# A two-layer decoder step on one core: squares summed before the product that averages them, gate rows in one pass, sample states outside the tiles

## The reference, cut to what matters

```
y = x * rsqrt(mean(x*x) + eps) * g                 # _rmsnorm, before every projection
proj = h @ w_in                                    # layer 0: 8 groups of 512 columns, and 8 gate columns
rq, rk, rv, rg, mq, mk, mv, mo, mi, mf = split(proj)
i_pre = mi + b_gates[:4];  log_f = log_sigmoid(mf + b_gates[4:])
S_new = S * chunk_dec + einsum('bhsk,bhsv->bhkv', kc * k_dec, vc)   # 4 retention heads
C_new = dec * C + einsum('bhsk,bhsv->bhkv', kc * w_end, vc)         # 4 mLSTM heads
x = x + concat(o_ret, h_m) @ w_out
x = x + swiglu(rmsnorm(x))                         # dense
# layer 1: HGRN2 mixer (8 heads), then top-2-of-8 SwiGLU experts on rmsnorm(x), then a last rmsnorm
```

## Time and profile before

| what | value |
|---|---|
| median of three runs | 1583.95 us (1582.96 to 1591.84) |
| span of the profiled execution | 1580.1 us, 23315 instructions |
| busy | PE 96%, PEld 84%, DVE 74%, ACT 58%, POOL 6% |
| granted TensorE clock, mean | 0.988 |
| DMA | 403.87 MB, mean 256 GB/s |

### The profile page before, as it was taken

How to read it: one execution, slowest core, us unless ns; L and a number is a source line. 1 busy time by engine, 2 the same in 40 slices (tenths; PEclk the granted TensorE clock), 3 DMA queues, 4 the chain that set the end, 5 groups by cost and what they waited for, 6 DMA issues and landing times.

```text
span 1580.1 us, 23315 instructions
## 1 busy us (share of the span) xinstructions
PE 1522.6 (96%) x8687; PEld 1333.2 (84%) x8687; DVE 1164.5 (74%) x1269; ACT 910.9 (58%) x905; POOL 87.7 (6%) x90
## 2 busy tenths in 40 slices
PE   6999998999999989998999999999999999999997
PEld 5888787999999988996778888888888888888885
DVE  5656566455454598686479898888988888898886
ACT  4334444434433544343277787877778787777773
POOL 0024100000000000102030000000000000000002
PEclk9999999999999999998999999999999999999999
DMA  7567723698545531444199999999999999999993
GB/s 206 149 112 142 144 74 94 184 301 261 144 129 153 180 103 54 127 132 142 64 384 359 402 391 364 386 360 390 379 388 384 364 385 363 398 386 372 393 353 126
DMA packets 214584, 403.87 MB, mean 256 GB/s; under 512 B 14467, under 2 KB 131503, under 8 KB 214386
## 3 DMA queue, kind: packets, MB, share of 16 engines
q1 hardware_dynamic: 203104, 372.82, 68.2%
q0 software_dynamic: 6208, 22.06, 4.5%
q10 hardware_dynamic: 5202, 8.03, 1.5%
HBM read 372.58 MB, written 30.28 MB: 255 GB/s over the span
## 4 chain that ended last, share of the span: by engine, by line
PE 86%; DVE 9%; ACT 2%; issue 1%; DMA 1%; ACTq 0%; DVEq 0%; SPq 0%
PE bank L483 25%; PE bank L484 24%; PE bank L485 24%; DVE dense_lo L1709 2%; PE bank L683 2%; PE bank L940 1%; PE bank L725 1%; PE bank L1089 1%; ACT dense_hi L1293 1%; PE bank L588 1%; DMA arena<-in_x_sample 1%; DVE w_lo L2218 1%; PE bank L675 1%; PE bank L620 1%; DMA ring<-in_w_in_c 0%
## 5 line engine op out<-in xcount | busy, mean ns | idle before, releaser
L2218 DVE TENSOR_TENSOR w_lo<-arena,w_hi 128x2048 fp32r<-128x2048 f32 (+1 forms) x280 | 597.1, 2166 | 84.7 <-ACT w_hi L1588 81.8
L1588 ACT ACTIVATE w_hi<-arena 128x2048 fp32r<-128x2048 f32 (+1 forms) x280 | 500.7, 1820 | 114.0 <-PE bank L485 113.0
L483 PE MATMUL bank<-w_hi,xg_hi 128*128 128x512 f32 (+1 forms) x768 | 287.5, 374 | 2.5 <-DVE w_lo L2218 2.3
L484 PE MATMUL bank<-w_lo,xg_hi 128*128 128x512 f32 (+1 forms) x768 | 286.1, 373 | 0.0
L485 PE MATMUL bank<-w_hi,xg_lo 128*128 128x512 f32 (+1 forms) x768 | 285.4, 372 | 0.0
L1709 DVE TENSOR_TENSOR dense_lo<-ring,dense_hi 128x2048 fp32r<-128x2048 f32 (+1 forms) x78 | 167.7, 2152 | 134.7 <-ACT dense_hi L1293 134.6
L1293 ACT ACTIVATE dense_hi<-ring 128x2048 fp32r<-128x2048 f32 (+1 forms) x78 | 140.6, 1804 | 179.4 <-PE bank L485 153.2
L483 PE MATMUL bank<-h_hi,dense_hi 128*128 128x320 f32 x512 | 170.2, 332 | 20.4 <-DVE h_lo_a L1715 7.8
L483 PEld LDWEIGHTS bank<-w_hi,xg_hi 128*128 128x128 f32 x768 | 144.5, 188 | 31.9 <-issue 4.3
L485 PEld LDWEIGHTS bank<-w_hi,xg_lo 128*128 128x128 f32 x768 | 144.2, 188 | 25.9
L484 PEld LDWEIGHTS bank<-w_lo,xg_hi 128*128 128x128 f32 x768 | 144.5, 188 | 24.9
(11 more groups left out here) (410 smaller groups left out, 2355.5 us busy)
## 6 DMA issues: line engine op xcount, KB each, us to landing
arena<-in_w_moe_down SPq DMA_DIRECT2D x176, 512.0 KB, 6.7
arena<-in_w_moe_gate SPq DMA_DIRECT2D x128, 512.0 KB, 6.7
arena<-in_w_moe_up SPq DMA_DIRECT2D x128, 512.0 KB, 7.0
arena<-in_w_moe_gate SPq DMA_DIRECT2D x64, 384.0 KB, 5.6
arena<-in_w_moe_up SPq DMA_DIRECT2D x64, 384.0 KB, 4.0
ring<-in_w_in_ab SPq DMA_DIRECT2D x32, 512.0 KB, 8.8
ring<-in_w_in_c SPq DMA_DIRECT2D x32, 512.0 KB, 4.7
expert_rows<-ZERO SPq DMA_DIRECT2D x12, 1024.0 KB, 8.2
```

The costliest lines, as they stand in the source:

```text
L483: mm(out, left[0], right[0], start=start, stop=False)
L484: mm(out, left[0], right[1], start=False, stop=False)
L1588: fn(WH[SLOT_OF[p]][:, 0:unit_size(p)], STAGE[:, s, 0:unit_size(p)], ACT.Copy).then_inc(S("unit_hi"), 1)
L2218: v.tensor_tensor(WL[w][:, 0:n], STAGE[:, s, 0:n], WH[w][:, 0:n].bitcast(F32), ALU.subtract).then_inc(S("unit_split"), 1)
```

## The change

- The eight squares of each norm are first summed on VectorE (`add_squares`, seven additions into tile 0; for n3 the first seven tiles, six additions), then one product (n3: two) with the 1/D matrix. The product's place is where the last two stood. The additions stand behind the low parts in VectorE's order, each waiting for the square and for the addition before it.
- `gates` makes one output of 36 rows: input gate columns at 0 to 3, forget gate columns at 32 to 35, zeros between. The two weight parts get a place in the arena that GpSimd zeroes at the start (two memsets); ScalarE fills the high part with two copies, VectorE the low part with two subtractions. ScalarE's `gate_rows` first copies the forget rows out of the bank, adds the bias to the input rows, then adds the bias to the forget rows in place.
- `along` is taken out before `state` of heads 0, 3, 4, 5 and 6. Their tile runs through, then the prompt's products, then the four sample products back to back.

```diff
-    silu0 mq3 along state0 wh wl wh state1 conv2 wl score2 ...
+    silu0 mq3 state0 wh wl wh state1 conv2 wl score2 ...
...
-    along weigh3 silu4 wl state2 conv4 mv0 conv5 mk3 along state3 conv6 wh silu5 shift4 wh mv1 ...
+    along weigh3 silu4 wl state2 conv4 mv0 conv5 mk3 state3 conv6 wh silu5 shift4 wh mv1 ...
...
-    conv7 center1 silu7 wl mv4 score4 mv5 mo0 weigh4 wh shift5 mo1 along state4 wl score5 wh center2 wl mo2
-    finish4 weigh5 finish5 center3 center4 conv_out rg0 along state5 center5 var0 root0 shift6 score6 mo3 weigh6
-    mix0 mix1 wh mix2 gate0 wl wh wl rg1 shift7 finish6 score7 mix3 gate1 rg2 along state6 rg3 along weigh7
+    conv7 center1 silu7 wl mv4 score4 mv5 mo0 weigh4 wh shift5 mo1 state4 wl score5 wh center2 wl mo2
+    finish4 weigh5 finish5 center3 center4 conv_out rg0 state5 center5 var0 root0 shift6 score6 mo3 weigh6
+    mix0 mix1 wh mix2 gate0 wl wh wl rg1 shift7 finish6 score7 mix3 gate1 rg2 state6 rg3 along weigh7
...
+            SUMMED = {"n1": 0, "n2": KD - 1, "n3": 2 * (KD - 1)}
...
             def mean_squares(tag):
                 b = open_bank("act")
+                if tag == "n3":
+                    pe.wait_ge(S("squares_summed"), SUMMED["n3"] + KD - 2)
+                    mm(b[:, 0:NT], C("inv_d"), SQF[tag][:, 0, :], start=True, stop=False)
+                    pe.wait_ge(S("n3_squares"), KD)
+                    ins = mm(b[:, 0:NT], C("inv_d"), SQF[tag][:, KD - 1, :], start=False, stop=True)
+                else:
+                    pe.wait_ge(S("squares_summed"), SUMMED[tag] + KD - 1)
+                    ins = mm(b[:, 0:NT], C("inv_d"), SQF[tag][:, 0, :], start=True, stop=True)
+                close_bank("act", ins, (tag, "ms"))
...
             def gates():
-                for r in range(2):
-                    b = open_bank("act")
-                    for k in range(KD):
-                        ins = product3(b[0:H4, 0:NT], [x[:, k, r * H4:(r + 1) * H4] for x in (WGH, WGL)],
-                                       [x[:, k, :] for x in HA], k == 0, k == KD - 1)
-                    close_bank("act", ins, ("gate", r))
+                b = open_bank("act")
+                for k in range(KD):
+                    ins = product3(b[0:GROW, 0:NT], [x[:, k, :] for x in (WGH, WGL)], [x[:, k, :] for x in HA],
+                                   k == 0, k == KD - 1)
+                close_bank("act", ins, "gate")
...
                     gemm_tile(w, k % 2 * P, src, "dve", (kind, k), KD)
-                    add(k - 2)
...
                 if f == 0:
-                    add(KD - 2)
-                    add(KD - 1)
+                    mean_squares("n1")
...
                 close_bank("dve", ins, ("fd", m))
-                if m >= 2:
-                    add(m - 2)
...
-                free(fn(I_R, take(("gate", 0))[0:H4, 0:NT], ACT.Identity, bias=gbias[:, 0:1]))
-                free(fn(Z_R, take(("gate", 1))[0:H4, 0:NT], ACT.Identity, bias=gbias[:, 1:2]))
+                b = take("gate")
+                n = step(fn(Z_R, b[32:GROW, 0:NT], ACT.Copy))
+                free(fn(I_R, b[0:H4, 0:NT], ACT.Identity, bias=gbias[:, 0:1]))
+                act.wait_ge(act_step, n)
+                fn(Z_R, Z_R, ACT.Identity, bias=gbias[:, 1:2]).then_inc(S("gate_rows"), 1)
...
+            def add_squares(tag, k):
+                total = SQF[tag][:, 0, :]
+                before = {"n1": 0, "n2": KD - 1, "n3": 2 * (KD - 1)}[tag]
+                dve.wait_ge(S(tag + "_squares"), k + 1)
+                if k > 1:
+                    dve.wait_ge(S("squares_summed"), before + k - 1)
+                v.tensor_tensor(total, total, SQF[tag][:, k, :], ALU.add).then_inc(S("squares_summed"), 1)
...
                     if k > 0 and lo is not None:
                         low(tag, k - 1, dst, lo, hi)
+                    if k > 1:
+                        add_squares(tag, k - 1)
                     if k % 2:
                         split_dense()
                 if lo is not None:
                     low(tag, KD - 1, dst, lo, hi)
+                    add_squares(tag, KD - 1)
                 scale_of(tag)
...
+            g.memset(WGH[:, :, :].bitcast(F32), 0.0).then_inc(S("zero"), 1)
+            g.memset(WGL[:, :, :].bitcast(F32), 0.0).then_inc(S("zero"), 1)
```

More of the change, by code:

```diff
@@ L361, in trunk_kernel @@
         V1 = sb("V1", [P, 3])
-        WGH, WGL = sb("wgate_hi", [P, KD, 2 * H4], F32R), sb("wgate_lo", [P, KD, 2 * H4], F32R)
+        GROW = 32 + H4
+        WGH, WGL = parts("wgate_hi", AT_ARENA + 20472, KD, GROW), parts("wgate_lo", AT_ARENA + 20472 + KD * GROW, KD, GROW)
         RND = sb("RND", [P, 4])
@@ L841, in _, with projection_out @@
             head_variances("hn0", 1)
-            def projection_out(kind, src, tag, heads):
+            def projection_out(kind, src, heads):
                 out = {"oab": "mix0_h", "oc": "mix1_h"}[kind]
@@ L970, in _ @@
                 elif name == "ms":
-                    add(KD - 2)
-                    add(KD - 1)
+                    mean_squares("n2")
                 elif name == "rt":
@@ L993, in _ @@
             head_variances("hn1", 1)
-            add = projection_out("oc", (HH, HL_O), "n3", "hn1")
+            projection_out("oc", (HH, HL_O), "hn1")
             pe.wait_ge(S("router_in"), 32)
@@ L1000, in _ @@
                 if k == 4:
-                    add(KD - 2)
-                    add(KD - 1)
+                    mean_squares("n3")
                 pe.wait_ge(S("n3_value"), k + 1)
@@ L1175, in _ @@
                 if 0 <= piece < NZERO:
-                    sp.wait_ge(S("zero"), 1)
+                    sp.wait_ge(S("zero"), 3)
                     flat = XD[CAP:(NBLOCK + 1) * CAP, :].rearrange("(p b) (r d) -> p (b r) d", p=P, d=256)
@@ L1315, in _ @@
             act.wait_ge(S("scales_one"), 1)
-            act.wait_ge(S("zero"), 1)
+            act.wait_ge(S("zero"), 3)
             fn(V1[:, :], ZERO[:, 0:3], ACT.Square)
@@ L1333, in _ @@
             act.wait_ge(S("wgate_in"), 16)
-            fn(WGH[:, :, :], wgate[:, :, :], ACT.Copy).then_inc(S("wgate_hi"), 1)
+            act.wait_ge(S("zero"), 3)
+            fn(WGH[:, :, 0:H4], wgate[:, :, 0:H4], ACT.Copy)
+            fn(WGH[:, :, 32:GROW], wgate[:, :, H4:2 * H4], ACT.Copy).then_inc(S("wgate_hi"), 1)
             act.dma_start(cst[:, NFIRST:], A["cst"][:, NFIRST:]).then_inc(S("tables_in"), 16)
@@ L1362, in gate_rows @@
                 act.wait_ge(act_step, n)
-                fn(L_R, L_R, ACT.Ln, bias=1.0).then_inc(S("gate_ln"), 1)
+                fn(L_R, L_R, ACT.Ln, bias=1.0).then_inc(S("gate_rows"), 1)
                 act.wait_ge(S("gate_exps_in"), 1)
@@ L1758, in gate_rows @@
             def gate_rows():
-                after_empty(dve, ("gate", 1))
+                after_empty(dve, "gate")
+                dve.wait_ge(S("gate_rows"), 1)
                 v.scalar_tensor_tensor(out=T_R, in0=Z_R, scalar=-1.0, in1=Z_R, op0=ALU.mult,
                                        op1=ALU.max).then_inc(S("gate_abs"), 1)
-                dve.wait_ge(S("gate_ln"), 1)
+                dve.wait_ge(S("gate_rows"), 2)
                 dve.wait_ge(S("rows_zero"), 2)
@@ L1904, in _ @@
                     dve.wait_ge(S("wgate_hi"), 1)
-                    v.tensor_tensor(WGL[:, :, :], wgate[:, :, :], WGH[:, :, :].bitcast(F32),
-                                    ALU.subtract).then_inc(S("wgate_split"), 1)
+                    for at, of in ((slice(0, H4), slice(0, H4)), (slice(32, GROW), slice(H4, 2 * H4))):
+                        ins = v.tensor_tensor(WGL[:, :, at], wgate[:, :, of], WGH[:, :, at].bitcast(F32), ALU.subtract)
+                    ins.then_inc(S("wgate_split"), 1)
                     split_dense()
@@ L2020, in _ @@
                     low("n2", k - 1, U_C, HL_C)
+                if k > 1:
+                    add_squares("n2", k - 1)
                 split_dense()
             low("n2", KD - 1, U_C, HL_C)
+            add_squares("n2", KD - 1)
             scale_of("n2")
```

15 lines of the change are left out of this document (3 added, 12 removed).

## The result

| | before | after |
|---|---|---|
| median (runs) | 1587.89 us (4; 1582.96 to 1595.55) | 1561.95 us (4; 1558.28 to 1566.6) |
| profiled execution | span 1580.1 us | total 1559.97 us, span 1558.2 us |
| granted clock, mean | 0.988 | 0.988 |

The ratio is 0.985, 95% interval 0.9814 to 0.9886: faster by 1.1 to 1.9%, at the time forecast (1562.5 us). The old median is higher here than ahead of the prediction because a fourth run of 1595.55 us joined the three; the difference of medians is 25.9 us here, and 22.9 and 20.1 us in two later groups of runs. The total of the profiled execution is 1.8 us above its span. So of the 3.85 us that the prediction set between the old span and the median only about half surrounds the span; the rest was the difference between one execution and the next.

The account below looks back on a forecast made before the run. TensorE, busy 96% of the span, was taken to bound the kernel. Gates 3.2, unweaving 9.9 and squares 8.4 sum to 21.5 us off 1580.1, plus 3.85 to the median: 1562.5 us; own range 1558 to 1567, whole range 1556 to 1574.

Parts of the forecast that it names:

- The gates, 3.2: Gate products at the start: 24 fewer save 3.5 us of TensorE; bounds 2.8 (through VectorE's split) and 3.5, taken as 3.2.
- The squares, 8.4: Three norms: 20 fewer mean-square products of 0.54 us, walked along the chain, give 8.4 us together; bounds 1.0 and 10.8.
- n1: Norm after the output projection: five products earlier, one addition on the path, one product for two; -3.0 us.
- n2: Norm at the dense stage's end: four products count, one addition on the path, one product for two; -2.2 us.
- n3: Norm at the router: six products count and the new wait costs nothing; -3.2 us.
- The term of +0.49: First two norms: the addition for tile 6 stands between first low part and VectorE's split, costing 0.49 us each.
- rival 2: Norms: the additions land on the path, so the squares give only 1 us; 1570 us in all, chance 0.07.
- rival 4: Clock: sharper TensorE waits bring two to four more lower-clock stretches, costing 3.4 to 6.8 us; 1566 to 1569.5, chance 0.09.
- The unweaving, 9.9: Input stage, five heads: running sample products together saves TensorE 2.2 us a head, 9.9 us after waits; bounds 0 and 12.1.
- Head 4: Input stage: TensorE's wait for a split behind VectorE's update grows from 1.2 to about 2.2 us; gain 1.2 us.
- the update ends 1.2 us earlier: Head 4's VectorE state update, starting later but no longer spread, ends 1.2 us earlier than before.
- Head 5: Input stage: nothing waits on the state update before TensorE's own work; gain 2.1 us.

Follow-up runs that it names:

- gates_only: Kernel before with only the gate rows made in one pass: 1578.63 us, ratio 0.9957.
- unweave_only: Kernel before with only the five heads' sample-state products unwoven: 1577.93 us, ratio 0.9941.
- wide_woven: Kernel before, still woven, with the five heads' sample products on 128 rows of other data in place of 32: 1571.66 us in a single run.
- addition_late: Changed kernel with the addition for tile 6 moved behind VectorE's split at the first two norms: 1571.43 us in a single run.
- state2_first: Changed kernel with head 2's state products moved ahead of tile mk2: 1565.31 us, ratio 0.9883.
- sum_only: Kernel before with only the norms' squares summed on VectorE: 1576.21 us, ratio 0.994.

## Why the prediction was right, point by point

**The total.** 1562.5 forecast, 1561.95 measured. That it came within 0.6 us is luck: 3.0 us too much was expected of the change in this execution, and 2.9 us of the old profile's span (the late start and the clock at 564 us) were nothing that the change could keep. The mechanisms of the three parts were right, except at head 4 and for the clock.

**The gates, 3.2.** Right: 3.2 in the kernel after, 3.5 alone. The unit at 60.99 in the earlier trace rows is taken at 56.65, 4.3 us earlier or 2.2 without the earlier start, TensorE waiting 1.12 us for it. The chain through VectorE's split was somewhat longer than the 2.8 us counted, but the bound that decided was the other: behind ScalarE's next split the full gain was back.

**The squares, 8.4.** Right: n1 2.9 (3.0), n2 2.2 (2.2), n3 3.5 (3.2), together 8.6, and 9.0 in medians alone. The term of +0.49 for the addition ahead of the split was 0.39 to 0.41. In the kernel after TensorE waits for the sum at none of the three norms; rival 2 falls with its price of 7.4 us. Two things the sum had left to rival 4, and they show only over all profiles. At n1 before itself ran at the lower clock. `gates_only`, `unweave_only` and `wide_woven`, with the same code there, did not, and for that alone gained 1.5 us on it from unit 19 to 22. Of the 10 profiles with the squares 9 have the lower clock there and gain about 2.8 us. Against an execution of before with full clock behind that wait the change gives only 1.3 us at n1. And at n2 the wait grew to between 1.9 and 3.2 us in the ten, from 1.0 to 1.2 in the four without the squares; six of the ten fall to the lower clock there and none of the four, and n2's share goes from -0.8 to 3.1 us. The 2.2 us of the kernel after, at full clock, are one of these.

**The unweaving, 9.9.** The saving of 2.2 us a head in TensorE was right, and so was its cause. The Trainium skill (TensorEngine Tiling (Array Packing), Key Properties) has that a change of tiling mode drains TensorE; the wide products agree, with 0.39 us for two changes. The rest of the saving, two narrow products at once, was not in the prediction's reasons. Head 0 gave 3.1 (3.2), head 3 1.6 (1.3), head 6 2.3 (2.1). Two terms failed:

- Head 4: the step "the update ends 1.2 us earlier" was mis-sized. It ended, and VectorE's next split began, 0.6 us earlier against the landmark before; TensorE's wait grew to 2.5 us, not 2.2, and 0.6 us were left.
- Head 5: 2.1 forecast, 1.0 in the kernel after, and 2.4 with the unweaving alone. What took 1.4 us is the clock behind head 4's wait (0.72). The prediction named this as rival 4 and gave it 0.09, with the argument that earlier waits of 2.00 and 1.23 us were followed by no slow stretch. The rows were read rightly, and the conclusion was wrong: six profiles have the wait of 2.5 us behind head 4; in the 4 us behind it the clock is 0.60, 0.64 and 0.61 in the three of the changed kernel, and 1.00 in those of `unweave_only`, `addition_late` and `state2_first`. One profile with full clock behind a wait does not show that the wait is safe.

**The lower clock.** Forecast and rival 4 both came about: the terms of the forecast, less 1.4 us at head 5 and 1.9 us at the end of the input stage (0.66 in 230 to 240 us; before had 0.66 from 235 to 240). The first is seen behind a wait that the change made longer; the second is not shown to be the change's, as `sum_only`, `gates_only` and `wide_woven` lost 2.7, 1.7 and 1.5 us there with woven heads. The Trainium skill (TensorE: Matmul & The Clock Gate, HAM oscillation) has that an idle gap that is long enough throttles the clock again, each time; the traces agree in that most of the low stretches of the input stage and the norms begin at a wait, but neither does each wait bring one nor does each stand at a wait (`gates_only`, 98.4 us).

**What was not foreseen.** That setting TensorE ahead in the input stage takes the slack of head 3's state load. The prediction looked at the stores and loads by their place in the order ("earlier or at most as late") and not at the time that remains between this load's issue and its use.

## What to carry to other kernels

When products leave a tile and run together, look at what the in-order engine behind them does next: here a background update stood before the split that TensorE waits for, and swapping the two was worth another 5 us. Small matmuls with another number of rows than their neighbours are dear where they alternate (here 0.39 us for going to 32 rows and back); put them together. A gain of 1 or 2% in a kernel whose lower-clock stretches come and go needs landmarks in several profiles: terms of 1 to 3 us can be read there and not in the totals.

## What the hardware did that I had not expected

- The clock behind a wait is not given by the wait. `addition_late` runs the changed kernel's instructions up to n1 and has head 4's wait at 2.51 us as well, with a clock of 1.00 in the 4 us behind it where the changed kernel has 0.60 to 0.64. And 24 us at a mean of 0.68 followed a wait of only 1.39 us. At head 1 the wait of 2.00 us is followed by full clock in before and by the lower one in `sum_only` and `wide_woven`. I found no row that tells beforehand which it will be.
- Float32 products of 32 rows, for two banks and from two groups of rows, ran side by side: pairs of records 0.014 us apart in before at head 1, four products in 1.07 us where one of 128 rows takes 0.43.
- A load of 512 KB issued at the same point of the program took 11.0 us in one execution and 9.4 in another, in the changed kernel both times.
- Unweaving alone has single times from 1569.0 to 1583.1 us. That is wide, though the gates alone (1574.5 to 1588.3) and before in the same group (1578.7 to 1593.9) are about as wide. Which stretch makes it so stays open, since its one profile (span 1567.2 us) is of the shortest.
- A reduced-format product costs TensorE 0.146 us with 4, 36 or 128 columns of weights.
